# Attention in one hybrid layer: turned probabilities and values multiplied unsplit in one four-byte product per tile

## What is computed

```python
def block_attention(q, k, v):
    b, lq, h, dh = q.shape
    nb = lq // Q_BLOCK
    grp = h // N_KV_HEADS
    qb = q.reshape(b, nb, Q_BLOCK, N_KV_HEADS, grp, dh).transpose(1, 0, 2, 3, 4, 5)
    scale = dh ** -0.5

    def one_block(qi):
        s = jnp.einsum("bqkgd,bskd->bkgqs", qi, k).astype(f32) * scale
        p = jax.nn.softmax(s, axis=-1).astype(v.dtype)
        return jnp.einsum("bkgqs,bskd->bqkgd", p, v)
...
```

## Time and profile before

| | us |
|---|---|
| median of 3 runs | 3129.18 (3128.32 to 3130.61) |
| profiled execution, its own time | 3127.13 |
| its span, first to last instruction | 3125.2 |
| PE busy | 2696.9 (86%) |
| DVE busy | 1910.4 (61%) |
| ACT busy | 827.9 (26%) |
| POOL busy | 120.6 (4%) |

### The profile page before, as it was taken

The page is one execution under the profiler, slowest core; times in us unless marked ns, Lnnn a source line. Parts: engine busy times, 40 slices in busy tenths (PEclk is TensorE's granted clock), DMA queues, the critical chain, the costliest instruction groups (busy, mean ns, idle before and its releaser), DMA issues. The chain is left out here.

```text
span 3125.2 us, 40178 instructions
## 1 busy us (share of the span) xinstructions
PE 2696.9 (86%) x16234; PEld 1748.9 (56%) x16234; DVE 1910.4 (61%) x2836; ACT 827.9 (26%) x1234; POOL 120.6 (4%) x141
## 2 busy tenths in 40 slices
PE   7899999999974749999588879748599999999993
PEld 7555555555532738888466657533255555555541
DVE  2577777785567277776254454557555555555559
ACT  0411111111103226666233343321321111111110
POOL 0000000000001030000000000001100000000002
PEclk9999999999985869999789889769699999999996
DMA  6223322311112100000210000021221111111102
GB/s 234 83 82 107 95 95 95 95 54 41 48 41 74 50 5 1 1 1 1 68 31 22 28 16 1 4 89 66 89 65 44 40 40 40 54 54 40 47 18 110
DMA packets 149704, 169.76 MB, mean 54 GB/s; under 512 B 7943, under 2 KB 124579, under 8 KB 148530
## 3 DMA queue, kind: packets, MB, share of 16 engines
q1 hardware_dynamic: 149554, 167.66, 16.8%
HBM read 152.79 MB, written 14.85 MB: 54 GB/s over the span
## 5 line engine op out<-in xcount | busy, mean ns | idle before, releaser
L672 PE MATMUL psum<-act_hi,ffn_win_hi 128*128 128x384 f16 x2112 | 690.3, 327 | 8.2 <-DVE ffn_win_lo L880 8.2
L672 PE MATMUL psum<-act_lo,ffn_win_hi 128*128 128x384 f16 x2112 | 690.3, 327 | 0.0
L672 PE MATMUL psum<-act_hi,ffn_win_lo 128*128 128x384 f16 x2112 | 690.2, 327 | 0.0
L806 ACT ACTIVATE ffn_silu<-psum,ffn_win_inverse 128x384 f32<-128x384 f32 x132 | 76.7, 581 | 1143.3 <-PE psum L672 1141.2
L700 PE MATMUL psum<-ffn_wout_hi,ffn_h_hi 128*128 128x512 f16 x792 | 314.8, 397 | 63.2 <-DVE Y L938 56.6
L938 DVE SCALAR_TENSOR_TENSOR Y<-psum,ffn_h_unit,Y 128x512 f32<-128x512 f32 x360 | 265.7, 748 | 117.3 <-PE psum L700 115.3
L700 PE MATMUL psum<-ffn_wout_lo,ffn_h_hi 128*128 128x512 f16 x792 | 313.9, 396 | 0.0
L700 PE MATMUL psum<-ffn_wout_hi,ffn_h_lo 128*128 128x512 f16 x792 | 312.7, 395 | 0.0
L672 PEld LDWEIGHTS psum<-act_hi,ffn_win_hi 128*128 128x128 f16 x2112 | 207.2, 98 | 144.2 <-DVE ffn_win_lo L880 8.5
L672 PEld LDWEIGHTS psum<-act_hi,ffn_win_lo 128*128 128x128 f16 x2112 | 207.1, 98 | 137.5 <-issue 1.5
L672 PEld LDWEIGHTS psum<-act_lo,ffn_win_hi 128*128 128x128 f16 x2112 | 207.1, 98 | 136.2 <-issue 1.0
(11 more groups left out here) (292 smaller groups left out, 4418.7 us busy)
## 6 DMA issues: line engine op xcount, KB each, us to landing
ffn_win_raw<-in_w_in SPq DMA_DIRECT2D x88, 512.0 KB, 5.0
w_mod<-in_w_mod SPq DMA_DIRECT2D x36, 1024.0 KB, 5.0
ffn_wout_raw<-in_w_out SPq DMA_DIRECT2D x44, 512.0 KB, 4.2
scan_w_raw<-in_w_mix SPq DMA_DIRECT2D x20, 512.0 KB, 4.0
x_after<-ffn_x_row SPq DMA_DIRECT2D x9, 512.0 KB, 2.6
mixout_residual<-x_after SPq DMA_DIRECT2D x9, 512.0 KB, 3.4
x_after<-mixout_x_row SPq DMA_DIRECT2D x9, 512.0 KB, 2.6
ffn_residual<-x_after SPq DMA_DIRECT2D x9, 512.0 KB, 3.4
```

The costliest lines, as they stand in the source:

```text
L672: last = nc.tensor.matmul(bank[:, 0:CH], win[b][w][:, half, k, :], K.A[a][:, k, c * CH:(c + 1) * CH], start=(n == 0), stop=(n == 3 * KT - 1))
L806: nc.scalar.activation(sa[s][:], pa[s][:, 0:CH], ACT.Silu, scale=winv[:, b:b + 1]).then_inc(silu, 1)
```

## The change

Probabilities and values are no longer split. A turned tile is copied once, as plain float32, into one of four buffers; even tiles are copied by ACT, odd tiles by DVE, each waiting for the turn and for the buffer. The values are used where they lie (`cv` for the two cached tiles, `K.V` for the rest), 64 columns wide, and a tile takes one four-byte product of 512 columns into the lower 64 partitions of `OB`. DVE copies these into `K.O` at the end of the unit. The split of the values, the copy of the upper part and the addition go. Keys and queries are split as before. As two engines now free the banks, there is a semaphore for each, and a list `order` of all turns gives each turn its place and count. On PE, value tiles 2, 3 and 4 stand one turn earlier than before.

The diff, cut to its core:

```diff
-        vs = place("v_hi_lo", [P, NKT, NKV, 2, DH], F32R)
...
-        pt = [[place(f"probsT_{i}_{x}", [P, HPK * P], F32R) for x in ("hi", "lo")] for i in range(NPT)]
+        pt = [place(f"probsT_{i}", [P, HPK * P]) for i in range(NPT)]
...
-        lowh = place("pv_low_half", [DH, HPK * P])
...
+        order = [("k", 0, 0), ("k", 0, 1), ("k", 0, 2), ("q", 0, 0), ("k", 1, 0), ("k", 1, 1), ("k", 1, 2), ("q", 1, 0)]
         for u in range(NU):
+            order += [("p", u, n) for n in range(min(8, tiles[u]))]
+            if u + 2 < NU:
+                order.append(("q", u + 2, 0))
+            order += [("p", u, n) for n in range(8, tiles[u])]
+        place_of = {x: i for i, x in enumerate(order)}
+        by_act = lambda x: x[0] == "p" and x[2] % 2 == 0
+        taken_at = {x: (from_act if by_act(x) else from_dve, sum(by_act(y) == by_act(x) for y in order[:i + 1]))
+                    for i, x in enumerate(order)}
+
+        def taken(eng, *x):
+            s, count = taken_at[x]
+            eng.wait_ge(s, count)
+
+        split_at = {x: sum(y[0] != "p" for y in order[:i + 1]) for i, x in enumerate(order)}
...
         def _(pe):
-            def bank_of(i):
+            def bank_of(*x):
+                i = place_of[x]
                 if i >= 2:
-                    pe.wait_ge(lo, i - 1)
+                    taken(pe, *order[i - 2])
                 return T[i % 2]
...
                 if u < 0 or n >= tiles[u]:
                     return
                 g = first[u] + n
-                pe.wait_ge(lo, turn_at[u, n] + 1)
+                taken(pe, "p", u, n)
                 if n == 0 and u:
-                    pe.wait_ge(added, u)
-                v = vs[:, keys(u)[n], u % NKV].rearrange("p x d -> p (x d)")
-                for x in range(2):
-                    last = nc.tensor.matmul(OB, v, pt[g % NPT][x][:], start=(n == 0 and x == 0),
-                                            stop=(n == tiles[u] - 1 and x == 1))
-                last.then_inc(pv, 1)
+                    pe.wait_ge(o_out, u)
+                kt, cols = keys(u)[n], slice(u % NKV * DH, (u % NKV + 1) * DH)
+                nc.tensor.matmul(OB[0:DH, :], cv[:, kt, cols] if kt < 2 else K.V[:, kt - 2, cols], pt[g % NPT][:],
+                                 start=(n == 0), stop=(n == tiles[u] - 1)).then_inc(pv, 1)
...
             main(0, 3)
-            pe.wait_ge(lo, key_at[1, 2] + 1)
-            pe.wait_ge(v_lo, 2)
+            pe.wait_ge(cache_in, 32)
+            taken(pe, "k", 1, 2)
             tails(1, 0)
             main(1, 0)
...
@@ -1399,13 +1392,13 @@
                 values(u, 1)
                 tails(u + 1, 1)
                 turn(u, 4)
+                values(u, 2)
                 turn(u, 5)
-                values(u, 2)
                 main(u + 1, 3)
+                values(u, 3)
                 turn(u, 6)
-                values(u, 3)
+                values(u, 4)
                 turn(u, 7)
-                values(u, 4)
                 values(u, 5)
                 turn_queries(u + 2)
                 values(u, 6)
...
-            def probs_hi(u, n):
+            def take(u, n):
                 if n >= tiles[u]:
                     return
-                i, g = turn_at[u, n], first[u] + n
+                i, g = place_of["p", u, n], first[u] + n
                 act.wait_ge(turned, i + 1)
                 if g >= NPT:
                     act.wait_ge(pv, g - NPT + 1)
-                nc.scalar.activation(pt[g % NPT][0][:], T[i % 2], ACT.Copy).then_inc(hi, 1)
+                nc.scalar.copy(pt[g % NPT][:], T[i % 2]).then_inc(from_act, 1)
 
...
-            def low_half(u):
-                act.wait_ge(pv, first[u + 1])
-                if u:
-                    act.wait_ge(added, u)
-                nc.scalar.copy(lowh[:], OB[DH:P, :]).then_inc(low_out, 1)
...
-            nc.scalar.activation(vs[:, 0:2, :, 0, :], cv[:].rearrange("p t (h d) -> p t h d", h=NKV), ACT.Copy).then_inc(v_hi, 1)
-            nc.scalar.activation(vs[:, 2:NKT, :, 0, :], K.V[:].rearrange("p t (h d) -> p t h d", h=NKV), ACT.Copy).then_inc(v_hi, 1)
             exponents(0, 3)
             exponents(1, 0)
             for u in range(NU):
-                probs_hi(u, 0)
-                probs_hi(u, 1)
-                probs_hi(u, 2)
+                take(u, 0)
                 exponents(u + 1, 1)
-                probs_hi(u, 3)
-                probs_hi(u, 4)
-                probs_hi(u, 5)
+                take(u, 2)
+                take(u, 4)
                 exponents(u + 1, 2)
-                probs_hi(u, 6)
-                probs_hi(u, 7)
+                take(u, 6)
                 exponents(u + 1, 3)
                 queries_hi(u + 2)
-                probs_hi(u, 8)
-                probs_hi(u, 9)
-                low_half(u)
+                take(u, 8)
                 exponents(u + 2, 0)
...
-            def probs_lo(u, n):
+                                               ALU.mult, ALU.subtract).then_inc(from_dve, 1)
+
+            def take(u, n):
                 if n >= tiles[u]:
                     return
-                i, g = turn_at[u, n], first[u] + n
-                dve.wait_ge(hi, i + 1)
-                nc.vector.tensor_tensor(pt[g % NPT][1][:], T[i % 2], pt[g % NPT][0][:].bitcast(F32), ALU.subtract).then_inc(lo, 1)
+                i, g = place_of["p", u, n], first[u] + n
+                dve.wait_ge(turned, i + 1)
+                if g >= NPT:
+                    dve.wait_ge(pv, g - NPT + 1)
+                nc.vector.tensor_copy(pt[g % NPT][:], T[i % 2]).then_inc(from_dve, 1)
 
...
-            def add_halves(u):
-                dve.wait_ge(low_out, u + 1)
+            def take_out(u):
+                dve.wait_ge(pv, first[u + 1])
                 kt0, t = HGH + 2 * (u % NKV), u // NKV
                 for par in range(2):
-                    heads = lambda x: x.rearrange("p (a b q) -> p a b q", b=2, q=P)[:, :, par, :]
-                    last = nc.vector.tensor_tensor(K.O[par * DH:(par + 1) * DH, kt0:kt0 + 2, t * P:(t + 1) * P],
-                                                   heads(OB[0:DH, :]), heads(lowh[:]), ALU.add)
-                last.then_inc(added, 1)
+                    last = nc.vector.tensor_copy(K.O[par * DH:(par + 1) * DH, kt0:kt0 + 2, t * P:(t + 1) * P],
+                                                 OB[0:DH, :].rearrange("p (a b q) -> p a b q", b=2, q=P)[:, :, par, :])
+                last.then_inc(o_out, 1)
...
-            dve.wait_ge(v_hi, 2)
-            nc.vector.tensor_tensor(vs[:, 0:2, :, 1, :], cv[:].rearrange("p t (h d) -> p t h d", h=NKV),
-                                    vs[:, 0:2, :, 0, :].bitcast(F32), ALU.subtract).then_inc(v_lo, 1)
-            nc.vector.tensor_tensor(vs[:, 2:NKT, :, 1, :], K.V[:].rearrange("p t (h d) -> p t h d", h=NKV),
-                                    vs[:, 2:NKT, :, 0, :].bitcast(F32), ALU.subtract).then_inc(v_lo, 1)
             inverses(0)
             least(1, 0)
             for u in range(NU):
-                probs_lo(u, 0)
                 least(u + 1, 1)
-                probs_lo(u, 1)
-                probs_lo(u, 2)
-                probs_lo(u, 3)
+                take(u, 1)
+                take(u, 3)
                 least(u + 1, 2)
-                probs_lo(u, 4)
-                probs_lo(u, 5)
+                take(u, 5)
                 least(u + 1, 3)
-                probs_lo(u, 6)
-                probs_lo(u, 7)
+                take(u, 7)
                 inverses(u + 1)
                 queries_lo(u + 2)
-                probs_lo(u, 8)
-                probs_lo(u, 9)
+                take(u, 9)
                 least(u + 2, 0)
-                add_halves(u)
+                take_out(u)
...
```

More of the change, by code:

```diff
@@ L1244, in attention_phase @@
         OB = banks[7]
-        cache_in, q_twice, v_hi, v_lo, turned, hi, lo = (
-            sem(n) for n in ("cache_in", "q_twice", "v_hi", "v_lo", "turned", "hi", "lo"))
+        cache_in, q_twice, turned, hi, from_act, from_dve = (
+            sem(n) for n in ("cache_in", "q_twice", "turned", "hi", "taken_by_act", "taken_by_dve"))
         k_twice = [sem(f"k_twice_{kv}") for kv in range(NKV)]
@@ L1261, in attention_phase @@
         first = [sum(tiles[:u]) for u in range(NU + 1)]
[L1263 to L1274, removed]
-        for u in range(NU):
[L1276 to L1282, removed]
+        order = [("k", 0, 0), ("k", 0, 1), ("k", 0, 2), ("q", 0, 0), ("k", 1, 0), ("k", 1, 1), ("k", 1, 2), ("q", 1, 0)]
+        for u in range(NU):
+            order += [("p", u, n) for n in range(min(8, tiles[u]))]
[10 more added lines that the diff above has]
+        split_at = {x: sum(y[0] != "p" for y in order[:i + 1]) for i, x in enumerate(order)}
         def score_view(u, s):
@@ L1303, in turn_keys @@
                     pe.wait_ge(k_twice[kv], 2)
-                bank = bank_of(key_at[kv, b])
+                bank = bank_of("k", kv, b)
                 for j, kt in enumerate(range(*KB[b])):
```

(23 more changed lines are left out.)

10 lines of the change are left out of this document (4 added, 6 removed).

## The result

The changed kernel takes 3217.32 us (median of 4, 3217.05 to 3217.93) against 3128.75 (median of 4, 3127.93 to 3130.61): a ratio of 1.0283, 95% interval 1.0265 to 1.0300. The forecast was slower by 44 us; it is slower by 88.6. The profiled execution took 3217.54 us, with a span of 3215.7.

The account below looks back on a forecast made before the run. PE bounds attention: a unit's 18.57 us of work plus 3.93 makes 22.50. Units 0 to 14 +43.2, start -0.15, unit 15 +2.1, units 16 and 17 -1.1: +44 us, median 3173, range 3164 to 3187.

Parts of the forecast that it names:

- the value product: On PE in attention, one four-byte product replaces two fp32r records: +0.393 us a tile, +3.93 us a unit.
- FFN 1's row products: Four-byte products with 512 moving columns, the price source: pitch 0.430 us, 0.860 us per product.
- The copies and waits: In attention, one copy per tile relieves DVE and ACT some 3 us each; PE's 0.97 us of waits a unit go whole.
- the moved calls: Value tiles 2, 3 and 4 one turn earlier on PE: cost nothing; without them turns would stand back to back and wait.
- PE's wait for the queries: In each unit of the kernel before, PE waits 0.46 us for the queries' low half.
- The start: PE's 6.08 us wait for the split of the values nearly stays, for unit 0's last exponential: gain 0.15 us.
- Unit 15 and the end: Attention's last units: unit 15 +2.1 us; units 16 and 17, the context block, -1.1 us over both.
- the one for a slower time: Attention waits stay or new ones come as copies miss turns: +8 to +15 us, 3181 to 3188; chance 11%.
- The rival in the clock: PE falls to the 1.2 GHz level inside attention: +30 us or more, 3200 and up; chance 4%.
- The figure of the Trainium skill: For the faster rival: 131 ns per 512-column matmul, 0.52 us per value product, total near 3120; chance 3%.

Follow-up runs that it names:

- experiment 1: The changed kernel with a stationary side of 128 columns (the wide side or wide load) instead of 64 in the value product: 3169.41 us.
- experiment 3: The changed kernel with value tiles in pairs on PE, so five blocks of narrow products a unit instead of nine: 3196.34 us.
- experiment 4: The changed kernel with PE's order of calls from the kernel before, value tiles 2, 3 and 4 one turn later, eight narrow blocks: 3215.89 us.
- experiment 5: The changed kernel with a stationary side of 96 columns in the value product: 3169.57 us.
- experiment 6: The changed kernel with a stationary side of 72 columns in the value product: 3170.74 us.
- experiment 7: The changed kernel with odd units' value product written to partitions 64 to 127 and copied out from there: 3219.45 us.
- experiment 2: The kernel before with 64 stationary columns, the values' high halves alone, still two fp32r products a tile: 3127.92 us.
- experiment 8: The changed kernel with turned tiles and values rounded to fp32r, one 64-wide fp32r product a tile, low halves left out: 3081.48 us.
- experiment 9: The kernel before with the turned queries' copies moved ahead of head 3's exponential on ACT and of the reciprocals on DVE: 3121.94 us.

## Why the prediction was wrong

The side was right, and so was what bounds the stage; the size was half of what came, and the median lies 30 us over the range.

- *The step that failed* is in the value product: "the weight loads now hide behind the record before them, and 64-wide loads will hide too". They do not, when the product is four-byte and 64 columns wide. The load into such a block starts only when the products in front are nearly through (at 1313.20, the turn's record ending at 1313.28), and the first load behind the block too (at 1314.21, the product's record ending at 1314.27; with the wide side at 1301.14, the record ending at 1301.73). That is 0.334 us a block, nine blocks, 3.01 us of the 3.10 that a unit was longer than forecast. Experiments 1 and 3 to 7 show it; that both conditions are needed, experiments 2 and 8. What PE does inside to hold these loads back stays open.
- I had priced the product from FFN 1's row products and taken the pitch among them. That is right for products in a row: with the wide load the unit comes to 22.59 us, forecast 22.50, and the median to 3169.4, forecast 3173. That the total agrees so well is in part luck: attention ends 45.4 us later there (1538.1 against 1492.7), and the scan, which I had taken as unchanged, is 3.9 us shorter. The row's own neighbours had given a hint of the passage, though they are f16 products and cannot tell its two conditions apart. This is the kernel before, in FFN 1, where that group begins:

```profile
248.08 0.10 PEld L672 LDWEIGHTS psum<-act_hi,ffn_win_lo 128*128 128x128 f16 x1
248.24 0.33 PE L672 MATMUL psum<-act_hi,ffn_win_lo 128*128 128x384 f16 x1
248.50 0.09 PEld L403 LDWEIGHTS psum<-mod_sums,row_pick 128*4 128x4 f32 x2 [0.32 <-issue]
248.50 1.02 PE L403 MATMUL psum<-mod_sums,row_pick 128*4 128x512 f32 x2
```

The load of the f16 product stands 0.16 us ahead of it. The four-byte load, 4 columns wide, stands at the product's own start, 0.26 us behind the last f16 product instead of 0.16. Behind the group it is the same: its last record starts at 251.50, the next product and its first load at 252.03, 0.53 us later instead of 0.43. I compared widths by pitch, 4 columns against 128, found them equal and wrote that width does not matter; it matters at the passage, which a pitch inside a group cannot show.
- *The copies and waits* came as forecast: PE itself was idle for no copy in 13 units, and ACT and DVE are relieved (9.0 and 10.9 us busy a unit). Of the moved calls I had said that turns would wait without them; experiment 4 shows no such wait, and they cost one passage more. The 0.46 us that I read as PE's wait for the queries is a row of a load; experiment 9 shows that PE had lost 0.28 there.
- *The start*: the wait of 6.08 us is there as 5.98, now put down to the exponential, a gain of 0.10 for 0.15 forecast.
- *Unit 15 and the end*: +5.16 against +2.1, the 3.06 between them about nine passages again (3.01); units 16 and 17 -1.84 against -1.1.
- *The rivals*: the one for a slower time put the loss into copies that come late, at 0.5 to 1 us a unit, and its sign was a period of 23 or more with idle time of PE before turns or products. The period is there, 25.60, the idle time is not. The rival in the clock named 3200 and up, which covers the time, but it did not occur: the granted clock was 1.00. The figure of the Trainium skill (TensorE: Matmul & The Clock Gate, the back-to-back issue gap) of about 131 ns for a 512-column matmul in a stream finds no support in any run here: fp32r records stood 233 ns apart, four-byte ones 430, and f16 ones of 512 columns in FFN 1 216.

## What to carry to other kernels

A price read from a group of like instructions holds inside the group; before using it between unlike neighbours, look at what stands on either side, and whether the first load of the group starts ahead of its product or with it. A four-byte product that stands between wide loads, as here, should have a stationary side of 72 columns or more; columns that nobody reads cost nothing, and are worth 48 us here. Idle time of a load is not PE's loss: compare the start of a load with that of its product, and the starts of the products with each other. Trading two fp32r products for one four-byte product took PE from 0.467 to 0.860 us a tile, and the relief of the copying engines did not pay that back in a stage that PE bounds, even with the wide side (22.59 us a unit against 19.54).

## What the runs showed of the hardware

- A four-byte product with 64 stationary columns, between turns and scores, costs 0.334 us a block beyond its 0.86; with 72, 96 or 128 columns nothing; a fp32r product at 64 columns costs nothing beside its own time either. The half of the array does not matter (3219.45 us against 3217.32). The mechanism inside PE was not shown, only that loads are not issued ahead across such a passage, and no width between 64 and 72, and none between 4 and 64, was run.
- A four-byte record of 512 columns takes 0.43 us at a granted clock of 1.00 with 4, 64 and 128 stationary columns, and there are two to a product; a fp32r product is one record of 0.233.
- A turn whose first load starts with it and not ahead of it takes 0.91 us to the scores behind it instead of 0.81 (experiment 9).
- A busy PE may hide such a loss: it showed 332.80 of 332.80 us while 12% of it (3.0 of 25.6 us a unit) was neither product nor wait.
